# Multiplying the pooling mix into the projection's columns once, instead of into every tile

## What is computed

```python
z = rms_norm(x, norm_a[i]) @ w_in_a[i]
u, gp, qm, gm = jnp.split(z, [POOL_W, 2 * POOL_W, 2 * POOL_W + MEM_W], axis=-1)   # POOL_W = 768
u_ext = jnp.concatenate([pool_prefix[i], u], axis=1)          # 15 earlier rows
# pool_mixer, for each of 4 groups of 192 columns, with windows w = 2, 4, 8, 16:
win = cs[:, PAD + 1:PAD + 1 + T, sl] - cs[:, PAD + 1 - w:PAD + 1 - w + T, sl]     # window sums of u_ext
d = win / cnt - u_new[:, :, sl]
outs.append(jnp.einsum('btc,cd->btd', d, mix_w[g]))
yp = concatenate(outs) * scale * jax.nn.silu(gp)
ym = memory_branch(qm, gm, ...)
x = x + jnp.concatenate([yp, ym], axis=-1) @ w_out_a[i]
new_pool.append(u_ext[:, -POOL_PAD:])                         # state: the last 15 rows of the unmixed u
```

## Time and profile before

| | us |
|---|---|
| median of 3 runs (1894.3 to 1898.0) | 1894.39 |
| span of the profiled execution, first to last instruction | 1892.5 |
| what lies around the span, against the median | 1.9 |
| prologue, up to the first projection of tile 0 | 126 |
| loop A, 8 tiles of 85.4 to 85.9 | 685.8 |
| sample rows of layer A | 67.8 |
| loop B, 8 tiles | 904.4 |
| sample rows of layer B | 108.5 |

### The profile page before, as it was taken

The page is one execution under the profiler, slowest core; times in us unless marked ns, Lnnn a source line. Parts: engine busy times, 40 slices in busy tenths (PEclk is TensorE's granted clock), DMA queues, the critical chain, the costliest instruction groups (busy, mean ns, idle before and its releaser), DMA issues.

```text
span 1892.5 us, 30310 instructions
## 1 busy us (share of the span) xinstructions
PE 1731.1 (91%) x12116; PEld 1351.4 (71%) x12116; DVE 772.5 (41%) x1628; ACT 474.5 (25%) x1177; POOL 489.5 (26%) x352
## 2 busy tenths in 40 slices
PE   6449999999999999989999999999999999999968
PEld 3338888888888888874776757677576776767755
DVE  1563232323233232322644637355373635537220
ACT  1443132221313132211412314132231313214110
...
GB/s 369 100 132 3 90 12 80 23 68 40 52 89 1 90 7 83 25 227 302 30 4 43 1 46 2 45 1 1 46 2 45 2 30 16 1 45 1 96 49 45
DMA packets 23851, 110.78 MB, mean 59 GB/s; under 512 B 3264, under 2 KB 3712, under 8 KB 13184
## 3 DMA queue, kind: packets, MB, share of 16 engines
...
## 4 chain that ended last, share of the span: by engine, by line
PE 45%; issue 36%; POOL 12%; DVE 4%; DMA 2%; ACT 2%; POOLq 0%; SPq 0%; ACTq 0%; DVEq 0%
PE ps_z L593 16%; PE ps_z L618 13%; POOL tiny_sb L1840 3%; POOL ph_sb L1969 3%; PE ps_z L669 3%; PE ps_z L609 2%; PE ps_z L732 2%; POOL pm_sb L1864 2%; POOL pm_sb L1875 2%; PE ps_p L795 1%; DVE w_in_sb L1371 1%; POOL big_sb L1845 1%; PE ps_t L559 1%; PE ps_s L630 1%; PE ps_z L582 1%
## 5 line engine op out<-in xcount | busy, mean ns | idle before, releaser
L593 PE MATMUL ps_z<-xn_sb,w_in_sb 128*128 128x256 f16 (+1 forms) x4752 | 499.0, 264 | 1.7 <-DVE gate_sb L1426 0.8
L593 PEld LDWEIGHTS ps_z<-xn_sb,w_in_sb 128*128 128x128 f16 x4752 | 425.0, 98 | 58.6 <-issue 6.8
L618 PE MATMUL ps_z<-gate_sb,w_out_sb 128*128 128x256 f32 x1920 | 425.3, 381 | 8.7 <-DVE gate_sb L1442 6.0
L618 PEld LDWEIGHTS ps_z<-gate_sb,w_out_sb 128*128 128x128 f32 x1920 | 361.6, 190 | 59.3 <-DVE gate_sb L1442 7.5
L1840 POOL TENSOR_TENSOR tiny_sb<-tiny_sb 128x2 f32<-128x2 f32 (+4 forms) x56 | 94.1, 1681 | 839.0 <-DVE tiny_sb L1393 546.4
L582 PE MATMUL ps_z<-w_in_sb,xn_sb 128*128 128x512 f16 (+2 forms) x840 | 181.7, 376 | 0.0
L1456 DVE TENSOR_TENSOR x_buf_sb<-x_buf_sb,ps_z 128x512 f32<-128x512 f32 x64 | 44.0, 688 | 292.6 <-PE ps_z L618 292.6
L582 PEld LDWEIGHTS ps_z<-w_in_sb,xn_sb 128*128 128x128 f16 (+1 forms) x840 | 82.8, 99 | 94.3 <-issue 0.3
L1041 ACT ACTIVATE scr_sb<-ps_z,tiny_sb 128x256 f32<-128x256 f32 (+2 forms) x94 | 42.5, 489 | 420.1 <-PE ps_z L582 317.1
L1384 DVE TENSOR_REDUCE tiny_sb<-scr_sb 128x8 f32<-128x512 f32 (+3 forms) x64 | 38.0, 593 | 251.3 <-ACT scr_sb L1041 156.5
L1229 ACT ACTIVATE ph_sb<-ph_sb,tiny_sb 128x128 f32<-128x128 f32 x192 | 74.7, 390 | 138.4 <-DVE tiny_sb L1682 138.4
...
## 6 DMA issues: line engine op xcount, KB each, us to landing
...
w_in_sb<-parts ACTq DMA_DIRECT2D x8, 1024.0 KB, 12.0
...
```

The lines of the kernel that those rows point to most:

```text
L593: last = mm(ps_z[:, b, half * NT:half * NT + n], w_split[:, g, ws, kc, half * P:(half + 1) * P], xs[:, x, kc, 0:n], start=(kc == 0 and ws ...
L618: last = mm(ps_z[:, b, half * NT:half * NT + n], w[:, g, kc, half * P:(half + 1) * P], src[:, kc, 0:n], start=(kc == 0), stop=(kc == KC - 1))
```

## The change

The mix is multiplied once, in the prologue, into the 768 columns of `w_in_a` that make `u`. TensorE computes these three groups from the transposed raw columns (`w_u_t`, 1 MB each) and the mix blocks (`mixed_weights`: six calls, in `ps_s`), and VectorE multiplies them by the norm gain as it takes them out of PSUM (`mixed`), in place of GpSimd's `first_gained`. The order in which the groups are prepared becomes `ORDER`: the five other groups of layer A come in places 0 to 4, the mixed ones in places 5 to 7. In the tiles the mix is gone from TensorE, and `mix_gated` reads the differences in SBUF; `project_out` waits for the new signal `pool_gated`. The row of reciprocal norms (`rb`) of loop A moves from ring `Z` to `V`.

For the sample rows, the old state rows are mixed by 14 products (`mixed_state`), and the unmixed rows that the outputs need (64 sample rows and the last 15 prompt rows, which the host now appends to the sample tile of `x`) come from three products of 8 blocks with the raw columns (`raw_inputs`), each 1 MB loaded through `stage_b` (`w_u`). The seven old rows of each sample's state go from input to output in one transfer.

```diff
+ORDER = [0, 4, 5, 6, 7, 1, 2, 3, 8, 9]
...
-            "A": ["qm", *U3, *G3, "gm", "mix0", "mix1", "mix2", *OUTS],
-            "SA": ["qm", *U3, *G3, "gm", "mix0", "mix1", "mix2", "out0", "rb", "out1"],
+            "A": ["qm", *U3, *G3, "gm", *OUT],
+            "SA": ["qm", *U3, "raw0", "g0", "raw1", "g1", "g2", "raw2", "gm", "out0", "rb", "out1"],
...
+            "pre": [f"wp{n}" for n in range(6)],
             "A": ["m0", "m1"],
-            "SA": ["m"],
+            "SA": ["st", "m"],
...
+            dma(w_x[:, 0:14 * P], io["mix"]).then_inc(mix_in, 16)
+            dma(raw[5], io["w_in_a"][2]).then_inc(raw_in[5], 16)
+            for g in (1, 2, 3):
+                dma(w_in[:, g, :], io["w_u_t"][g - 1]).then_inc(raw_in[g], 16)
...
+            dma(stage_b, io["w_u"][0]).then_inc(wu_in, 16)
             sp.wait_ge(outputs, 4 * 16)
...
-            for n in range(12):
+            for n in range(4):
                 load_slot(sp, "SA", n, 0, 1)
+            Z.wait_full(sp, "SA", 0, "raw0")
+            dma(stage_b, io["w_u"][1]).then_inc(wu_in, 16)
+            for n in range(4, 12):
+                load_slot(sp, "SA", n, 0, 1)
+            Z.wait_full(sp, "SA", 0, "raw1")
+            dma(stage_b, io["w_u"][2]).then_inc(wu_in, 16)
             for n in range(12, 16):
                 load_slot(sp, "SA", n, 0, 1)
...
+            def mixed_weights(i, half):
+                if half == 0:
+                    for g in range(1, 4) if i == 1 else (1 + i, 2 - i // 2):
+                        pe.wait_ge(raw_in[g], 16)
+                b = S.wait_free(pe, "pre", 0, f"wp{2 * i + half}")
+                for k in range(4):
+                    kc = half * 4 + k
+                    for o in (2 * i, 2 * i + 1):
+                        ins = [c for (oo, c) in mix_blocks if oo == o]
+                        for c in ins:
+                            last = mm(ps_s[:, b, k // 2, (k % 2) * 256 + (o % 2) * P:(k % 2) * 256 + (o % 2 + 1) * P],
+                                      w_u_t[:, c, kc * P:(kc + 1) * P], mix_w[:, mix_blocks.index((o, c)), :],
+                                      start=(c == ins[0]), stop=(c == ins[-1]))
+                last.then_inc(S.full[b], 1)
...
+            def raw_inputs(g):
+                pe.wait_ge(raw_x, 1)
+                pe.wait_ge(wu_in, 16 * (g + 1))
+                b = Z.wait_free(pe, "SA", 0, f"raw{g}")
+                for kc in range(KC):
+                    last = mm(ps_z[0:NS + PAD, b, 0:256], big[:, kc, 0:NS + PAD], stage_b[:, kc, :],
+                              start=(kc == 0), stop=(kc == KC - 1))
+                last.then_inc(Z.full[b], 1)
...
-                    mix("A", t, NT)
                     largest("A", t, 0, "top0")
...
-                    Z.wait_read(pe, "A", t, "mix2")
+                    pe.wait_ge(pool_gated.sem, pool_gated.after("A", t))
                     project_out("A", t, (0,))
...
             def magnitudes(part, t, k, src, beside):
-                act.wait_ge(w_gained.sem, w_gained.after(part, t, k))
+                if part == "pre" and 5 <= k < 8:
+                    S.wait_read(act, "pre", 0, f"wp{2 * k - 10}")
+                    S.wait_read(act, "pre", 0, f"wp{2 * k - 9}")
...
+                dve.wait_ge(d_in.sem, d_in.after(part, t))
+                for c in range(POOLC):
+                    src, g = pooled(c)[:, 16:UW], gate[:, c, 0:n]
...
+                    last = ve.scalar_tensor_tensor(g, src, mix_scale[:, c:c + 1], g, ALU.mult, ALU.mult)
+                last.then_inc(pool_gated.sem, 1)
...
+            def mixed(i):
+                dve.wait_ge(low_in.sem, low_in.after("pre", 0, 2 + i))
+                for half in range(2):
+                    b = S.wait_full(dve, "pre", 0, f"wp{2 * i + half}")
+                    rows = gain[:, 0, half * 4:half * 4 + 4].rearrange("p (k n) -> p k n", n=1).to_broadcast([P, 4, 256])
+                    last = ve.tensor_tensor(stage_a[(5 + i) % 3][:, half * 4:half * 4 + 4, :],
+                                            ps_s[:, b].rearrange("p r (k n) -> p (r k) n", k=2), rows, ALU.mult)
+                    last.then_inc(S.free[b], 1)
...
             scale(3)
+            mixed(0)
             x_variance(T, "pre", 0, "ss")
             for g in range(4, 10):
                 start(g)
                 scale(g)
                 end(g - 1)
+                if g in (4, 5):
+                    mixed(g - 3)
...
-            for g in range(5, 10):
-                first_gained(g)
+            for j in (8, 9):
+                first_gained(j)
```

More of the change, by code:

```diff
@@ L255, in build @@
         mix_w = w_x[:, 0:14 * P].rearrange("p (n m) -> p n m", n=14)
+        mix_blocks = [(o, i) for o in range(POOLC) for i in range(POOLC)
+                      if o // 3 == i // 3 and abs(o - i) < 2]
+        w_u_t = w_in[:, 1:4, :].rearrange("p g (c k) -> p (g c) k", c=2)
+        raw_out = ph[:, 5408:5408 + 768].rearrange("p (g n) -> p g n", g=3)
         qT_b = ph[:, 0:2048].rearrange("p (c t) -> p c t", c=8)
@@ L330, in build @@
         PTM = ["ptm00", "ptm01", "ptm10", "ptm11"]
-        OUTS = ["out0", "out1", "rb", "out2", "out3"]
+        RAW = ["raw0", "raw1", "raw2"]
         W6 = [(0, 0), (1, 0), (0, 1), (1, 1), (0, 2), (1, 2)]
@@ L565, in rstd_rows @@
                 pe.wait_ge(diag_x.sem, diag_x.after(part, t, k))
-                ring = V if part == "B" else Z
+                ring = V if part in ("A", "B") else Z
                 b = ring.wait_free(pe, part, t, name)
-                out = ps_p[:, :] if part == "B" else ps_z[:, b]
+                out = ps_p[:, :] if ring is V else ps_z[:, b]
                 for blk in range(NBLK):
@@ L651, in mem_values @@
                 last.then_inc(V.full[0], 1)
-            def mix(part, t, n):
-                pe.wait_ge(mix_in, 16)
-                pe.wait_ge(d_in.sem, d_in.after(part, t))
-                blocks = [(o, i) for o in range(POOLC) for i in range(POOLC)
-                          if o // 3 == i // 3 and abs(o - i) < 2]
-                for pair in range(3):
-                    b = Z.wait_free(pe, part, t, f"mix{pair}")
-                    for o in (2 * pair, 2 * pair + 1):
-                        ins = [i for (oo, i) in blocks if oo == o]
-                        for i in ins:
-                            src = pooled(i)[:, 16:UW] if n == NT else \
-                                pooled(i)[:, 0:DB * US].rearrange("p (b t) -> p b t", b=DB)[:, :, 16:US]
-                            out = ps_z[:, b, (o % 2) * NT:(o % 2) * NT + n]
-                            if n != NT:
-                                out = out.rearrange("p (b t) -> p b t", b=DB)
-                            last = mm(out, mix_w[:, blocks.index((o, i)), :], src,
-                                      start=(i == ins[0]), stop=(i == ins[-1]))
-                    last.then_inc(Z.full[b], 1)
+            def mixed_weights(i, half):
[12 more added lines that the diff above has]
+                last.then_inc(S.full[b], 1)
@@ new lines, in mixed_state @@
+            def mixed_state():
+                pe.wait_ge(state_in, 16)
+                b = S.wait_free(pe, "SA", 0, "st")
+                for o in range(POOLC):
+                    ins = [c for (oo, c) in mix_blocks if oo == o]
+                    for c in ins:
+                        last = mm(ps_s[:, b, o // 4, (o % 4) * P:(o % 4) * P + DB * PAD], mix_w[:, mix_blocks.index((o, c)), :],
+                                  state_tmp[:, c].rearrange("p b t -> p (b t)"),
+                                  start=(c == ins[0]), stop=(c == ins[-1]))
+                last.then_inc(S.full[b], 1)
@@ L817, in _ @@
                 split_features("SA", 0, f"u{i}", 1 + i, NS)
+            mixed_state()
             q_transposes_a("SA", 0, NS, 1)
+            raw_inputs(0)
             T.wait_read(pe, "SA", 0, "qT")
             sample_mem_scores("SA", qbd_a, 1)
-            for i in range(3):
-                split_features("SA", 0, f"g{i}", 4 + i, NS)
+            split_features("SA", 0, "g0", 4, NS)
+            raw_inputs(1)
+            split_features("SA", 0, "g1", 5, NS)
+            split_features("SA", 0, "g2", 6, NS)
+            raw_inputs(2)
             split_features("SA", 0, "gm", 7, NS)
@@ L1201, in _, with raw_rows @@
                 last.then_inc(Z.free[b], 1)
+            def raw_rows(g):
+                b = Z.wait_full(act, "SA", 0, f"raw{g}")
+                f(raw_out[0:NS + PAD, g, :], ps_z[0:NS + PAD, b, 0:256], ACT.Copy, scale=1.0 / X_UNIT)\
+                    .then_inc(Z.free[b], 1)
             act.wait_ge(qbd_zero.sem, qbd_zero.after("SA", 0))
```

137 lines of the change are left out of this document (78 added, 59 removed).

## The result

The change makes the kernel slower: 1941.64 us (median of 4 runs, 1940.31 to 1944.59) against 1896.20 (1894.30 to 1898.11), a ratio of 1.0252 with a 95% interval of 1.0236 to 1.0269. The prediction was 1917.3, with a range up to 1932. The direction was right, and the time lies 9.6 us above the range.

The account below looks back on a forecast made before the run. It took TensorE to bound loop A, a chain round four engines the prologue, and no single engine to be named for the sample rows; -8.1 + 17 + 14 = +22.9 on 1892.5 gave 1915.4, forecast as 1917.3 us, range 1900 to 1932.

Parts of the forecast that it names:

- Part 1: Loop A: a gain, but only a third of the mix's time; net -8.1 us, between -20.1 and +3.9.
- mix gone, `rb` moved: Loop A: output projection starts 2.17 us earlier, moving `rb` saves 0.34; 2.51 us a tile, 20.1 in eight tiles.
- clock after the gap: Loop A: TensorE's clock falls after the idle gap, costing 1.5 us in each of eight tiles, 12.0 in all.
- No rival: Five other outcomes: clock holds (15%), slow prologue products (13%), sample rows hide loads (13%), faster (5%), tiles not shorter (9%).
- My upper bound of 3.0 a tile: Loop A: the clock's cost per tile if it stays down twice as long as the 1.5 us assumed.
- The gap: Loop A: TensorE idle for 4.84 us before the output projection in each tile, but for one `largest`.
- The prologue: Before tile 0: the added mixed-weight products and `mixed` steps lengthen the path by +17 us, bounds +11 to +40.
- The sample rows: Sample rows of layer A: raw products, their loads and waits outweigh the mix removed; +14 us, between +5 and +20.
- Layer B: Instructions unchanged, term 0; loop B's low clock stretches may fall elsewhere, a few times 1.5 us either way.

Follow-up runs that it names:

- x4b: x1 plus 9 products of 128x256 in each tile of loop A, read by nobody, to fill TensorE's idle gap: 1909.26 us.
- x1: Changed kernel with two waits exchanged in loop A: TensorE asks for the free scores bank ahead of its wait for the copied queries: 1927.35 us.
- x2: Changed kernel with one more wait on GpSimd in loop A: its second window sum waits for the first block's `m_neg`: 1927.31 us.
- x8: Changed kernel with 48 of the prologue's 112 mixed-weight products, only the diagonal blocks (wrong results): 1932.14 us.
- x12: x10 with the prologue's sixth `largest` moved ahead of the last 40 mixed-weight passes in TensorE's queue: 1862.67 us.
- x10: x6 with `weight_top` also ahead of `gm`'s gate and the first output products of chunks 0 to 5 not waiting for the memory gate: 1865.46 us.
- x6: x1 with VectorE's six `mix_gated` steps moved ahead of the silu of `gm` in loop A: 1900.41 us.

## Why the prediction was wrong

**Loop A, the step that failed.** Part 1 said that "without the mix the same chain runs up to 264.72, since nothing in it waits for the mix", and that "the other queues of the tile are not touched". I followed that chain only from the place of the edit onwards. The first half of the tile did change, through a ring that the prologue now uses and a wait value that takes one more addition. Put against the experiments, the term was:

| piece of loop A | predicted | measured | from |
|---|---|---|---|
| mix gone, `rb` moved | -20.1 | -20.2 | x4b (665.5) against before (685.7) |
| clock after the gap | +12.0 | +18.9 | x1 (684.4) against x4b |
| first transposes wait | none | +14.6 | changed kernel (699.0) against x1 |
| sum | -8.1 | +13.3 | |

The missed wait is the larger error. No rival held it, and the earlier trace rows could not show it, since they begin behind the scores. The gain agrees to 0.1 us, but in part by luck. The second tile of x4b shows this in its chain of waits; the single row under it is the start of the next tile in the kernel before:

```profile
271.08 5.36 PE ps_z L615 x48
281.57 7.17 PE ps_z L640 x32
...
310.36 5.41 PE ps_z L783 x48
```

```profile
298.69 5.41 PE ps_z L732 x48
```

From `gm`'s end to the output products it is 5.13 us where I had 4.84, so the mix brings 1.88 us a tile and not 2.17. From there to the next tile it is 28.79 us, before 29.39 (269.30 to 298.69), so the rest of the tile brings 0.60 where I had 0.34 for `rb`.

Of the block itself the rows show this: the 128x4 step lasts as long as GpSimd's sum that began just ahead of it (2.44 beside 2.42 us), and 0.17 us when it begins first. The reduction just ahead of it, which reads PSUM, takes 1.23 us while GpSimd's first sum runs, and 1.21 to 1.23 in the other rows looked at. The Trainium skill (SBUF — State Buffer, Who interferes with whom) gives the rule: VectorE and GpSimd share one pair of ports, `tensor_scalar` is among the steps that can take it, `tensor_reduce` on trn2 is not, and "Issue order, not op shape, decides who blocks". The trace agrees, and x2 shows the order deciding: 0.17 us beside the same late scores, once GpSimd comes second.

The block could have been read from the trace of the kernel before. The second `m_neg` of each tile took 1.18 us there, behind the same sum. In the prologue a step that spreads a largest weight took 3.62 us, where a like one takes 0.28, behind a multiply of GpSimd's that had begun 0.17 us earlier:

```profile
90.44 3.71 POOL L1869 TENSOR_TENSOR ph_sb<-w_in_sb,small_sb 128x2048 f32<-128x2048 f32 x1 [2.29 <-DVE w_in_sb L1371]
90.61 3.62 DVE L1347 TENSOR_SCALAR lo_sb<-small_sb,tiny_sb 128x128 f32<-128x128 f32 x1
```

The prediction used such a row for one step of the prologue (L1371, 4.38 us against 2.34) and did not ask where else a step stands close to one of GpSimd's.

**The clock.** The mechanism was right and the size too small. I took 1.5 us a tile from the earlier trace rows, where the low clock met four transposes and six passes. Here it meets 32 passes without a break. The first output products of the changed kernel in tile 0 and in tile 1:

```profile
200.57 8.79 PE L640 MATMUL ps_z<-gate_sb,w_out_sb 128*128 128x256 f32 x32 [2.72 <-DVE gate_sb L1509]
...
287.12 9.88 PE L640 MATMUL ps_z<-gate_sb,w_out_sb 128*128 128x256 f32 x32 [2.73 <-DVE gate_sb L1509]
```

The stretch just behind the first row's start, with the granted clock ahead of the last two columns:

```profile
202.00:203.00 1.00, 1.00 (x4) 0.82 (x3) 0.00 (x0) 0.66 (x1) 0.00 (x0) 0.50 0.00 0
```

That is the lower of the two levels, 1.2 GHz. Against 7.17 in the earlier trace rows the two rows are 1.6 and 2.7 us more; over the eight tiles the mean is 2.2, and without the wait at the transposes (x1) 2.4. My upper bound of 3.0 a tile held the mean.

**The gap** was predicted at 4.84 us, from `gm`'s end to the output products; in tile 0 it is 5.1 (195.47 to 200.57).

**The prologue** was right in sum and in mechanism; that the sum came out to a tenth is partly luck, since the same prologue took 140.9 to 146.3 us in eight profiles. The sixth `largest` ended at 109.55, where the prediction had 109.9, and tile 0 started at 142.91. Two pieces of that path:

```profile
66.83 10.97 PE L686 MATMUL ps_s<-w_x_sb,w_in_sb 128*128 128x128 f32 x80
...
98.09 6.32 PE L686 MATMUL ps_s<-w_x_sb,w_in_sb 128*128 128x128 f32 x40 [4.82 <-DVE ph_sb L1547]
```

The first 80 took 10.97 us where I had summed 10.8; after VectorE's `mixed` TensorE was idle for 4.82 us, where I had 4.6. x8 shows that the products set the time, and x12 that part of it is only their place in the queue.

**The sample rows** were right within 0.8 us in this profile; kernels with the same rows took 82.6 to 85.4 us, so this is partly luck as well. The two waits of the changed kernel:

```profile
862.73 3.86 PE L818 MATMUL ps_s<-x_buf_sb,ph_sb 128*32 128x256 f32 x16 [4.52 <-DMA x_buf_sb<-mem_ks]
...
881.12 6.33 PE L709 MATMUL ps_z<-w_x_sb,big_sb 128*79 128x256 f32 x16 [6.73 <-issue]
```

The third raw product waited 6.73 us and then ran mostly at the low clock (6.33 in place of 3.66); I had 5.7 and 2.4. Up to the end of the memory scores the stage grew by 7.1 us where I had summed 5.6, with the caches' wait at 4.52. From the memory values to the output projection it fell by 8.4, where I had 6.7. These errors cancel in part.

**Layer B** lost 2.0 us, inside what the prediction allowed for clock stretches that fall elsewhere.

## What to carry to other kernels

Where a change adds uses to a ring or a semaphore, look at every wait on it, not only those near the edit: a value that now needs one more instruction can shift a chain by less than 0.1 us. Then look for short steps on that chain that slip in just ahead of a long one on the engine beside it, and make the long one wait (x2), so that the order no longer hangs on luck. And a step taken off the bounding engine pays only once what stood in its shadow has moved too: here the change by itself lost 45 us, and with four steps reordered (x10) it won 28.

## What the runs showed of the chip

- A step on four numbers per partition took 2.44 us in place of 0.17, because GpSimd's sum had started 0.02 us ahead of it; a delay of 0.08 us a tile became 14.6 us of loop A.
- Nine products a tile that nobody reads, put into TensorE's idle time, made loop A 18.9 us shorter (x1 to x4b). Without the idle stretch ahead of the output products (x10) the granted clock in loop A was 1.00 without them.
- A gap of 2.4 us in all, with one `largest` in it (x6), still led to the lower of the two clock levels in seven tiles of eight.
